# Two unused strips of SBUF ahead of the activation halves in a two-block transformer kernel on one core

## The reference, cut to what matters

```python
x = x + mix(rms_norm(x, g))                               # mix: recurrence, then attention
x = x + square(relu(rms_norm(x, g) @ w_up)) @ w_down      # 1024 -> 4096 -> 1024, twice
z = h @ w_in                                              # second block, 1024 -> 8704
m = ga * (ya @ w_out_a) + gb * (yb @ w_out_b) + gc * (yc @ w_out_c)
x = x + gate * (m @ w_o)
```

## The kernel before, in words

| tensor | start | over 1 KB | tensor | start | over 1 KB |
|---|---|---|---|---|---|
| `raw` | 16512 | 128 | `xh` | 105152 | 704 |
| `whi` | 32896 | 128 | `xl` | 117440 | 704 |
| `wlo` | 49280 | 128 | `cx`, `xr`, `gt` | 129728 | 704 |
| `hch` | 88768 | 704 | `hhi` | 137920 | 704 |
| `hcl` | 96960 | 704 | `hlo` | 170688 | 704 |

## Time and profile before

### The profile page before, as it was taken

How to read it: one execution, slowest core, us unless ns; L and a number is a source line. 1 busy time by engine, 2 the same in 40 slices (tenths; PEclk the granted TensorE clock), 3 DMA queues, 4 the chain that set the end, 5 groups by cost and what they waited for, 6 DMA issues and landing times.

```text
span 919.5 us, 17949 instructions
## 1 busy us (share of the span) xinstructions
PE 876.0 (95%) x6992; PEld 829.3 (90%) x6992; DVE 705.5 (77%) x1076; ACT 443.3 (48%) x636; POOL 204.5 (22%) x220
## 2 busy tenths in 40 slices
PE   7998999999999996999999999998999999899998
PEld 5997899999899995599999999988799999899998
DVE  4767688899787689668767677785658998996793
ACT  7672344434443446645455434343357646543741
POOL 6221432224422100022222212241203313110000
PEclk9998999999999998899999999998999999999999
DMA  9752586667899642035666666554446544355442
GB/s 345 233 200 79 163 314 226 212 220 247 260 260 256 182 132 99 1 105 190 209 191 198 197 193 187 181 177 160 160 138 189 171 158 150 136 186 183 163 160 92
DMA packets 46960, 167.86 MB, mean 183 GB/s; under 512 B 5776, under 2 KB 5920, under 8 KB 46640
## 3 DMA queue, kind: packets, MB, share of 16 engines
q1 hardware_dynamic: 40896, 146.82, 47.9%
q0 software_dynamic: 5856, 20.00, 8.0%
q10 hardware_dynamic: 144, 0.15, 0.1%
HBM read 165.50 MB, written 1.44 MB: 182 GB/s over the span
## 4 chain that ended last, share of the span: by engine, by line
PE 63%; DVE 24%; issue 5%; ACT 5%; DMA 2%; SPq 1%; DVEq 0%; ACTq 0%; POOL 0%
PE bank L565 17%; PE bank L566 17%; PE bank L567 17%; DVE wlo L1305 7%; PE bank L629 3%; ACT whi L968 2%; DVE ada_prod L1478 2%; DMA raw<-weights 2%; DVE ada_prod L1454 2%; PE bank L647 2%; DVE xl L1324 1%; PE bank L789 1%; DVE tq L1509 1%; PE bank L883 1%; DVE score L1601 1%
## 5 line engine op out<-in xcount | busy, mean ns | idle before, releaser
L1305 DVE TENSOR_TENSOR wlo<-raw,whi 128x1024 fp32r<-128x1024 f32 x260 | 322.3, 1272 | 86.4 <-ACT whi L968 84.4
L565 PE MATMUL bank<-xh,whi 128*128 128x256 f32 x1328 | 376.1, 283 | 11.8 <-DVE vv L1724 3.4
L566 PE MATMUL bank<-xl,whi 128*128 128x256 f32 x1328 | 370.6, 279 | 0.0
L567 PE MATMUL bank<-xh,wlo 128*128 128x256 f32 x1328 | 370.5, 279 | 0.0
L968 ACT ACTIVATE whi<-raw 128x1024 fp32r<-128x1024 f32 x260 | 266.3, 1052 | 122.2 <-PE bank L567 101.7
L565 PEld LDWEIGHTS bank<-xh,whi 128*128 128x128 f32 x1328 | 250.6, 189 | 23.5 <-issue 8.3
L566 PEld LDWEIGHTS bank<-xl,whi 128*128 128x128 f32 x1328 | 250.6, 189 | 0.2
L567 PEld LDWEIGHTS bank<-xh,wlo 128*128 128x128 f32 x1328 | 250.5, 189 | 0.0
L565 PE MATMUL bank<-hhi,whi 128*128 128x256 f32 x512 | 142.8, 279 | 3.6 <-DVE wlo L1305 3.5
L567 PE MATMUL bank<-hhi,wlo 128*128 128x256 f32 x512 | 142.2, 278 | 0.0
L566 PE MATMUL bank<-hlo,whi 128*128 128x256 f32 x512 | 142.0, 277 | 0.0
(11 more groups left out here) (278 smaller groups left out, 1085.7 us busy)
## 6 DMA issues: line engine op xcount, KB each, us to landing
raw<-weights SPq DMA_DIRECT2D x260, 512.0 KB, 4.4
ada_raw<-ada_w POOLq DMA_DIRECT2D x24, 512.0 KB, 4.0
plain<-plain_w SPq DMA_DIRECT2D x16, 512.0 KB, 6.6
relB<-rel_scratch POOLq DMA_DIRECT2D x8, 256.0 KB, 8.0
bl<-rpb_in POOLq DMA_DIRECT2D x32, 64.0 KB, 3.6
x<-x_in SPq DMA_DIRECT2D x4, 256.0 KB, 6.2
cond<-cond_in POOLq DMA_DIRECT2D x1, 1024.0 KB, 7.2
cx<-ctx_in POOLq DMA_DIRECT2D x1, 1024.0 KB, 7.5
```

The lines of the kernel that those rows point to most:

```text
L565: mmul(dst, hi, rh, start=start, stop=False)
L566: mmul(dst, hi, rlo, start=False, stop=False)
L567: return mmul(dst, lo, rh, start=False, stop=stop)
L1305: V_.tensor_tensor(wlo[:, sl], raw[:, sl], whi[:, sl].bitcast(F32), ALU.subtract)\
```

## The change

Two tensors are allocated that no instruction uses: 12 float32 (48 bytes) in each partition ahead of `xh`, kept for the whole program, and 64 float32 (256 bytes) ahead of `hhi`, in the scope of the feed-forward tensors.

```diff
         hch = sb("hch", [P, DT, S], F32R)
         hcl = sb("hcl", [P, DT, S], F32R)
+        sb("gap_xh", [P, 12])
         xh = sb("xh", [P, 12, S], F32R)
         xl = sb("xl", [P, 12, S], F32R)
...
         cx = sb("cx", [P, DT, S])

         with ExitStack() as room:
+            sb("gap_hhi", [P, 64], F32, room)
             hhi = sb("hhi", [P, FT, S], F32R, room)
             hlo = sb("hlo", [P, FT, S], F32R, room)
             tq = sb("tq", [P, 2, 2, S], F32, room)
```

## The result

The changed kernel takes 932.68 us (median of five executions, 931.02 to 933.26), the kernel before, executed beside it, 921.25 us (five, 917.88 to 926.81). The ratio is 1.0115, with a 95% interval of 1.0078 to 1.0152: slower by 1.15%. The prediction was 924.0 us and a range of 911 to 930, so the time lies above the range. The profiled execution of the changed kernel has a span of 931.3 us, 11.8 us more than that of before.

A forecast was written before the change was run, and what follows sets the result against it. The prediction took the pace of TensorE's three matmul passes (51.1% of the chain) to bound the kernel. Every term was 0 on the profiled 921.22 us; centring four known draws of the pace gave 924.0 us, range 911 to 930.

The forecast's parts named there:

- What bounds the kernel: TensorE, busy 95% of the span: its three matmul passes make up 51.1% of the chain, 470 us of 919.5.
- Two paces, chosen at a pause: Matmuls step at 117.8 or 113.3 ns, each pace lasting until TensorE next pauses; all slow 929.0 us, all fast 910.7.
- The term of the matmuls: Matmuls with `xh`, `xl`, `hhi`, `hlo` at new offsets: taken as 0, bounded by -10.5 and +7.8 us.
- The second argument: Weight blocks already shift the distance between TensorE's two streams by 512 bytes, and steps don't go in two sizes with it.
- The bound: Matmul pace: best the fast pace everywhere, -10.5 us; worst the slow pace everywhere, +7.8 us; beyond that a further 4.5 ns step.
- rival C: New distances add another 4.5 ns to each moved pair's matmul: 122.3 ns, +26 us, 947 us; chance 0.05 with anything like it.
- the two signs named for C: In the changed kernel's TensorE profile: a third pace value above 117.8 ns, or LDWEIGHTS that take longer.
- The chance of slower: Whole kernel slower by over 1%: 0.05, against 0.77 for within 1% and 0.18 for faster by over 1%.
- VectorE, ScalarE and the transfers: Work on moved tiles taken as 0: engine instructions between -0.7 and +0.7 us, a `plain` load -0.4 to +0.4 us.
- Rival A: Place decides the matmul pace and the new distances choose the fast one: 911 to 916 us, chance 0.16.
- Rival B: New distances always choose the slow matmul pace, 117.8 ns: 929.0 us, 0.3% above the median; chance 0.05.
- Rival D: SBUF layout: the 48 bytes become 64, so `xh` moves by 64; outcome that of the forecast, sharing its 0.74.

The follow-up runs named there:

- `hhi_only`: Kernel before with only the 256-byte strip ahead of `hhi`, `xh` staying in place: 926.78 us, ratio 1.0037.
- `all_move`: Kernel before with a 64-byte strip ahead of `raw`, so weights and all three activation pairs move together: 922.64 us, ratio 0.9991.
- `raw_apart`: Kernel before with 64 unused bytes between `raw` and `whi`, so `raw` stays while weight halves and pairs move together: 920.30 us, one execution.
- the first four experiments: Kernel before with the strip ahead of `xh` alone (932.64 us), ahead of `hhi` alone (926.78), 64 bytes ahead of `raw` (922.64), 64 between `raw` and `whi` (920.30).
- `fine5`: Kernel before with distances to the weight blocks over 128 bytes set to 24 (`hch`), 68 (`xh`) and 116 (`hhi`): 943.77 us, ratio 1.0209.
- The kernels with unequal halves: Kernel before with 64-byte strips ahead of `wlo` and `x` (929.76 us), `wlo` alone (926.58), each lo half and next pair (931.31), or each activation half (934.98).
- `whi_moved`: Kernel before with 64 bytes ahead of `wlo` only, so `wlo` and all pairs move against `whi`: 926.58 us timed, ratio 1.0072.
- `fine1`: Kernel before with distances to the weight blocks over 128 bytes set to 48 (`hch`), 80 (`xh`) and 72 (`hhi`): 936.63 us, ratio 1.0131.
- `fine2`: Kernel before with distances to the weight blocks over 128 bytes set to 16 (`hch`), 56 (`xh`) and 112 (`hhi`): 932.76 us, ratio 1.0073.
- `spread`: Kernel before with strips of 32 bytes ahead of `hch`, 64 ahead of `xh` and 32 ahead of `hhi`: 926.35 us, ratio 1.0023.
- `xh_moved`: Kernel before with 64 unused bytes ahead of every activation half, hi halves at 0 and lo halves at 64 over 128 bytes: 934.98 us, ratio 1.0155.

## Why the prediction was wrong, point by point

*What bounds the kernel* held. The chain after, to be held against the earlier trace rows (shares of the span by line):

```profile
by line: PE bank L567 17.7%; PE bank L569 17.3%; PE bank L568 17.3%; DVE wlo L1307 6.7%; issue 4.9%; PE bank L631 3.0%; DMA raw<-weights 2.3%; ACT whi L970 2.2%; DVE ada_prod L1480 2.1%; DVE ada_prod L1456 1.5%; PE bank L649 1.5%; DVE xl L1
```

It goes by the three lines at 52.3% (51.1% before), and nearly all of the loss lies in a stretch that the prediction had marked as theirs. The worth of a step of pace in the block from 426 us on held too: 6.7 ns more on its 1507 matmuls came out as 10.0 us at the stage border.

*Two paces, chosen at a pause* held for the kernel before. In `hhi_only`, `all_move` and `raw_apart`, which read as before, the block in 435:495 ran once at 117.8 and twice at 113.3, and 31 executions of before beside the first four experiments lie between 917.19 and 928.83 us, within the 910.7 to 929.0 worked out for it. Of the 35 beside the later ones two lie above that, at 929.39 and 929.55.

The record shows more than the prediction read from four times. Sorted by the mean clock granted to each, these 66 executions of before fall into two groups at one and the same clock: at 0.991 they take 917.2 to 918.1 us or 924.4 to 924.5, at 0.989 they take 918.7 to 920.6 or 926.1 to 927.1, and at 0.985 they take 922.1 to 922.3 or 928.2 to 929.6. At these clocks and at 0.987 the groups are 6.4 to 6.8 us apart in the mean, and they have 34 and 32 members. That is the 6.7 us which the prediction put on the block from 426 us on running at one pace or the other, and the four traces with the old distances go with it: with the block at 113.3 they took 920.30, 920.33 and 921.22 us, with the block at 117.8 they took 925.79. The other 4 to 5 us of the scatter go with the granted clock, and not with the choice.

*The term of the matmuls* is the step that failed: "I take 0, the value that the row nearest to it gives, the pair of stretches with equal places and unequal pace." Two paces at one offset show that the offset doesn't choose between them. They don't show that it has no hand in what the two are. The runs show that it sets the pair of values, and that after a pause one of them is kept: 113.3 or 117.8 at a distance of 64, 118.7 or 120.0 at 0. The rows could not tell, since all three pairs stood at one offset, and the prediction said so; it then gave the forecast 0.74 all the same. The second argument, that 512 bytes between neighbouring blocks make no difference, was right as a reading, but a period of 128 divides 512, so it says nothing of 64.

*The bound.* Its worst end, 929.0 us, was the slow pace of before everywhere. In rival C a new step was named, priced at 4.5 ns on top of the slow pace, 122.3 ns and 947 us. The kind was right and the size wrong: on top of 117.8 came 0.9 or 2.2 ns. With the 4056 matmuls of the chain (the few with `hch` counted in) at 118.7 to 120.0 the prediction's own sum gives 921.2 + 4056 x 118.7 / 1000 - 470 = 932.7 us, or 937.9 us at 120.0, and the measured 932.68 stands at its lower end. That it fits so well is luck in part: in the profiled pair the block from 426 us on ran at 120.0 and cost 10.0 us, where the lower end has 8.1, and all the rest cost 1.8 us, where it has 3.3. The cases B and C left a gap from 929 to 936 in which the time fell. Of the two signs named for C the first came, a third value above 117.8; the weight loads of `xh` took 187 to 188 ns in 435:495 before and 188 to 190 after. What bad distances can cost was nearer to C than the change shows: `fine5` took 943.77.

*The chance of slower* was 0.05. Against the median of the three executions shown before (926.52) the loss would have been 0.7%; beside five, two of them new, that median was 921.25 and the ratio 1.0115. The prediction knew that the median was one draw of the choice of pace and set its centre by four draws, at 923.9. With two groups of nearly equal size that centre lies in the gap between them: the median was 923.58 in one set of 31 executions and between 919.69 and 926.35 in the smaller sets.

*VectorE, ScalarE and the transfers* held. The tap line has 468/477/484 ns after where the earlier trace rows has 471/478/484, and `plain` lands after 6.7 us against 6.6.

*Rival A* fell: no distance made the fast pace the only one, and only the old distance has it. *Rival B* fell too, as 117.8 is gone from the moved pairs. *Rival D*, that 48 bytes act as 64, held as to the layout, and it is these 64 bytes that cost the time.

*The two rules.* The Trainium skill ("TensorE: Matmul & The Clock Gate", Step-by-step: what each phase is for) says that loading the next weights takes no read bandwidth from the running matmul. By that rule the distance should be worth nothing, and the runs disagree in this much: with the clock, the instructions and the address of `xh` the same, a change of 64 bytes in where the weight blocks lie moved the step from 113.3 or 117.8 to 118.7 or 120.0 ns. The gap of 109.2 ns at 256 columns by the same page (Back-to-back issue gap) was reached nowhere; the lowest lasting pace in any run was 113.3. The prediction should not have called that a disagreement: the section gives its formula for an isolated matmul and says that in a stream of weight loads and matmuls both set the spacing, and every matmul here has its own weight load.

*What stays open.* Why a distance has the paces it has, and what at the pause picks one of them, isn't shown. That the two reads get in each other's way inside SBUF is the natural reading of a dependence on their distance alone, but it is argued, not shown: no run took one of the two reads away. The kernels with unequal halves refute the simplest form of it.

## What to carry to other kernels

When TensorE is on the chain in long unbroken stretches, take its pace start to start and compare stretches of one shape: a few ns there are 10 us over a kernel. The layout of SBUF is part of the kernel's speed then, so an edit that adds, drops or resizes a tensor ahead of the operands can move the time by 1 to 2% with no change in the work; an experiment that adds a buffer should keep the distance over 128 bytes between moving and stationary operand, or its result is mixed with this. And a quantity that never varied in the trace (here the offset of all three pairs) has no row that prices it: two outcomes at one value bound nothing about other values, and the range must say so. A median of a few executions of such a kernel is a draw as well: beside `whi_moved` 14 of 17 executions of before were in the faster group, beside `fine1` and `fine2` 2 of 9.

## What the runs showed of the hardware

- The step between back-to-back matmuls of 256 columns in fp32r, each with its own weight load, depends on the start of the moving tile less that of the weight block, over 128 bytes: 113.3 or 117.8 ns at 64; 118.7 or 120.0 at 0; 117.1 at 112; 121.6 to 122.2 at 68; 118.9 or 122.8 at 116. Moves by 128 (`hhi` in `spread`) and 256 bytes (`hhi_only`) change nothing, nor does moving both together by 64 (`all_move`).
- At one distance there can be two or three lasting paces. One is taken up after a pause and kept for as long as 1507 matmuls; which one differs from execution to execution. At 64 the choice in one block splits 66 executions of the kernel before into two groups 6.4 to 6.8 us apart at equal mean clock; with 4 to 5 us more that go with a mean clock of 0.993 to 0.985 they spread over 917.19 to 929.55 us.
- Within a lasting pace the steps can repeat with a period of three passes (117, 120, 123 ns in the changed kernel; 119, 124, 120 in `xh_moved`), so a mean over a window hides them.
- The duration of a matmul in the profile follows the pace by a few ns only (276 ns in 435:495 of before, at 113.3, and 279 or 280 in the same window of `all_move`, at 117.7), while the number of matmuls in a window shows it plainly.
